# Opening stage of a two-block transformer kernel: two of eight row blocks by float32r passes, context read last, x normed before its modulation, squares folded by additions

## What is computed

```python
m_lat = (jax.nn.silu(c) @ ada_w[l] + ada_b[l])[:, None]
m_ctx = jax.nn.silu(c_ctx) @ ada_w[l] + ada_b[l]
sh1, sc1, g1, sh2, sc2, g2 = jnp.split(m_lat, 6, axis=-1)
csh1, csc1, cg1, csh2, csc2, cg2 = jnp.split(m_ctx, 6, axis=-1)
h_lat = rmsnorm(x, norm_g[l, 0]) * (1.0 + sc1) + sh1
h_ctx = rmsnorm(ctx_s, norm_g[l, 0]) * (1.0 + csc1) + csh1
z = h @ w_in
```

## Time and profile before

| | |
|---|---|
| median of three runs | 3205.82 us (3204.47 to 3207.77) |
| profiled execution | 3206.09 us, span 3204.3 us |
| PE busy | 3103.4 us, 97% of the span |
| DVE, ACT, POOL busy | 1615.0, 949.7, 1656.5 us |
| first matmul of `first_pair` | 48.07 us after the start |
| first matmul of chunk 2 | 67.78 us after the start |

### The profile page before, as it was taken

The page is one execution under the profiler, slowest core; times in us unless marked ns, Lnnn a source line. Parts: engine busy times, 40 slices in busy tenths (PEclk is TensorE's granted clock), DMA queues, the critical chain, the costliest instruction groups (busy, mean ns, idle before and its releaser), DMA issues.

```text
span 3204.3 us, 40755 instructions
## 1 busy us (share of the span) xinstructions
PE 3103.4 (97%) x15496; PEld 2574.4 (80%) x15496; DVE 1615.0 (50%) x2488; ACT 949.7 (30%) x1707; POOL 1656.5 (52%) x880
## 2 busy tenths in 40 slices
PE   8998889999999998999999999999999999999998
PEld 4887778888999766888878888788888788888887
DVE  4897768722332775211147767435531466645521
ACT  3124431111353463111122355322211314732210
POOL 2441045666787404566646633466665663066664
PEclk9999999999999999999999999999999999999999
DMA  5531026632454201233222211233332222033231
GB/s 221 191 124 44 9 84 244 241 117 88 149 180 153 66 7 66 72 98 104 99 76 92 93 46 40 66 98 93 98 110 89 89 96 68 10 97 95 94 110 67
DMA packets 84552, 319.29 MB, mean 100 GB/s; under 512 B 9200, under 2 KB 10864, under 8 KB 83376
## 3 DMA queue, kind: packets, MB, share of 16 engines
q1 hardware_dynamic: 84400, 317.20, 30.1%
HBM read 315.06 MB, written 2.10 MB: 99 GB/s over the span
## 4 chain that ended last, share of the span: by engine, by line
PE 83%; DVE 8%; issue 3%; ACT 2%; DMA 2%; POOL 1%; SPq 0%; DVEq 0%; POOLq 0%; ACTq 0%
PE two L388 15%; PE two L390 15%; PE two L389 15%; PE two L537 7%; PE two L538 7%; PE two L539 7%; DMA ada_raw<-ada 2%; PE two L2460 1%; DVE ada_junk L1120 1%; PE two L1729 1%; PE two L3060 1%; PE two L3062 1%; PE two L3061 1%; PE two L2595 1%; PE two L2620 1%
## 5 line engine op out<-in xcount | busy, mean ns | idle before, releaser
L388 PE MATMUL two<-h_hi,w_hi 128*128 128x512 f32 x2096 | 824.6, 393 | 1.8 <-DVE h_lo L2341 1.0
L390 PE MATMUL two<-h_hi,w_lo 128*128 128x512 f32 x2096 | 815.7, 389 | 0.0
L389 PE MATMUL two<-h_lo,w_hi 128*128 128x512 f32 x2000 | 778.4, 389 | 0.0
L303 POOL TENSOR_TENSOR w_lo<-w_raw,w_hi 128x1024 fp32r<-128x1024 f32 x292 | 713.5, 2445 | 41.5 <-ACT w_hi L414 11.7
L297 POOL TENSOR_SCALAR w_hi<-w_raw 128x1024 fp32r<-128x1024 f32 x272 | 291.7, 1073 | 666.4 <-issue 322.1
L388 PEld LDWEIGHTS two<-h_hi,w_hi 128*128 128x128 f32 x2096 | 393.6, 188 | 88.8 <-issue 3.9
L390 PEld LDWEIGHTS two<-h_hi,w_lo 128*128 128x128 f32 x2096 | 393.5, 188 | 81.9
L389 PEld LDWEIGHTS two<-h_lo,w_hi 128*128 128x128 f32 x2000 | 375.6, 188 | 77.9 <-issue 1.4
L505 POOL TENSOR_SCALAR w_hi<-w_raw 128x1408 fp32r<-128x1408 f32 (+1 forms) x104 | 132.5, 1274 | 426.7 <-PE two L539 308.2
L509 POOL TENSOR_TENSOR w_lo<-w_raw,w_hi 128x1408 fp32r<-128x1408 f32 (+1 forms) x110 | 327.0, 2974 | 40.0 <-DVE z L2223 16.5
L537 PE MATMUL two<-hid_hi,w_hi 128*128 128x512 f32 x704 | 274.1, 389 | 0.0
(11 more groups left out here) (633 smaller groups left out, 5713.6 us busy)
## 6 DMA issues: line engine op xcount, KB each, us to landing
w_raw<-w_f0u SPq DMA_DIRECT2D x88, 512.0 KB, 3.6
row_raw<-ada SPq DMA_DIRECT2D x48, 512.0 KB, 4.4
w_raw<-w_ssm SPq DMA_DIRECT2D x48, 512.0 KB, 3.5
w_raw<-w_f0d SPq DMA_DIRECT2D x32, 704.0 KB, 4.0
w_raw<-w_f1u SPq DMA_DIRECT2D x44, 512.0 KB, 3.5
w_raw<-w_f2u SPq DMA_DIRECT2D x44, 512.0 KB, 3.5
w_raw<-w_f3u SPq DMA_DIRECT2D x44, 512.0 KB, 3.5
ada_raw<-ada SPq DMA_DIRECT2D x32, 512.0 KB, 3.6
```

Of the source, the lines that this page charges most:

```text
L303: nc.gpsimd.tensor_tensor(lo[:, 0:self.kt], w_raw[j][:, 0:self.kt], hi[:, 0:self.kt].bitcast(f32), ALU.subtract).then_inc(split_done, 1)
L388: nc.tensor.matmul(dst, w_h[:, k], hi, start=kk == 0, stop=False)
L389: nc.tensor.matmul(dst, w_h[:, k], lo, start=False, stop=False)
L390: last = nc.tensor.matmul(dst, w_l[:, k], hi, start=False, stop=kk == self.parts * self.kt - 1)
```

## The change

It touches only the work up to the end of `first_pair`. Row blocks 4 and 6 are split: ACT rounds each quarter to float32r, DVE subtracts, and PE multiplies both parts by four columns `c_four` (the silu columns rounded, and the rest of their rounding). Every row result has four rows now, so the turn is done by f32 matmuls with a 4 x 2 matrix `row_pair` that adds rows in pairs, in place of transposes. `x` is read one block later, the first two weight chunks are read in `Start`, and the context comes behind them. DVE folds the squares of `x` by three additions and multiplies `x` by its reciprocal root in advance (`x_norm`). `FirstApply` lets ACT form `h_hi` from `x_norm` directly, and puts the context's squares between; POOL folds them, and PE sums them inside `first_pair` behind latent tile 5. ACT rounds weight chunk 0.

```diff
+                        if not (isinstance(i, int) and RAW * i + j < self.preloaded):
+                            sp.dma_start(w_raw[j][:, 0:self.kt], src).then_inc(raw_ready[j], 16)
...
+                        if isinstance(i, int) and n == SPL:
+                            self.side.pool(pool)
...
+                        if (not self.hi_act or a == 0) and not (isinstance(i, int) and n < self.rounded):
...
+                            if rhs is self.rhs:
+                                self.side.pe_first(pe, k)
...
+        SPLIT_ROWS = (4, 6)
...
             def sp(self, sp):
                 for k in range(ND):
-                    if k == 2:
+                    if k == 3:
                         sp.dma_start(x[:, :, :], xT.rearrange("(k p) t -> p k t", p=P)).then_inc(self.x_in[0], 16)
-                    if k == 4:
-                        sp.dma_start(xc[:, :, :], ctxT.rearrange("(k p) t -> p k t", p=P)).then_inc(self.xc_in[0], 16)
                     sp.dma_start(ada_n[k][:], ada0n[k:k + 1].rearrange("o p f -> (o p) f")).then_inc(self.w_in[k][0], 16)
+                for j in range(2):
+                    sp.dma_start(w_raw[j][:, 0:8], self.w[j:j + 1].rearrange("o p k f -> (o p) k f")).then_inc(raw_ready[j], 16)
+                sp.dma_start(xc[:, :, :], ctxT.rearrange("(k p) t -> p k t", p=P)).then_inc(self.xc_in[0], 16)
...
             def pe(self, pe):
-                pe.wait_ge(*upto(self.c_ready, 1))
+                pe.wait_ge(*upto(self.c_ready, 3))
                 for k in range(ND):
-                    pe.wait_ge(*upto(self.w_in[k], 16))
+                    split = k in SPLIT_ROWS
+                    if not split:
+                        pe.wait_ge(*upto(self.w_in[k], 16))
                     for q in range(4):
-                        last = nc.tensor.matmul(ps[q][0:2, :], c_silu[:, k], ada_n[k][:, 512 * q:512 * q + 512], start=k == 0, stop=k == ND - 1)
-                        if k == ND - 1:
-                            last.then_inc(self.in_ps[0], 1)
+                        cols = slice(512 * q, 512 * q + 512)
+                        if split:
+                            pe.wait_ge(*upto(self.hi, self.piece(k, q)))
+                            nc.tensor.matmul(ps[q][0:4, :], c_four[:, k], ada_hi[k][:, cols], start=False, stop=False)
+                            pe.wait_ge(*upto(self.lo, self.piece(k, q)))
+                            nc.tensor.matmul(ps[q][0:4, :], c_four[:, k], ada_lo[k][:, cols], start=False, stop=False)
+                        else:
+                            last = nc.tensor.matmul(ps[q][0:4, :], c_full[:, k], ada_n[k][:, cols], start=k == 0, stop=k == ND - 1)
+                            if k == ND - 1:
+                                last.then_inc(self.in_ps[0], 1)
                     if k == 4:
                         pe.wait_ge(*upto(self.folded, 1))
-                        nc.tensor.matmul(ps[6][:], ones[:], x_sum[:], start=True, stop=True).then_inc(self.sums[0], 1)
-                    if k == 6:
-                        pe.wait_ge(*upto(self.folded, 2))
-                        nc.tensor.matmul(ps[7][:, 0:TC], ones[:], xc_sum[:], start=True, stop=True).then_inc(self.sums[0], 1)
+                        nc.tensor.matmul(ps[6][:], ones[:], x_sq[:, 0], start=True, stop=True).then_inc(self.summed[0], 1)
                 for q in range(4):
                     pe.wait_ge(*upto(self.copied, q + 1))
                     for n in range(4 * q, 4 * q + 4):
-                        last = nc.tensor.transpose(ps[4][:, 2 * n:2 * n + 2], ada_row[:, n * P:(n + 1) * P], ident[0:2, 0:2])
+                        last = nc.tensor.matmul(ps[4][:, 2 * n:2 * n + 2], ada_row[:, n * P:(n + 1) * P], row_pair, start=n == 0, stop=True, skip_group_check=True)
...
+            def ctx_sum(self, pe):
+                pe.wait_ge(*upto(self.c_folded, 3))
+                nc.tensor.matmul(ps[7][:, 0:TC], ones[:], xc_sq[:, 0], start=True, stop=True).then_inc(self.c_summed[0], 1)
+            def pool_fold(self, pool):
+                pool.wait_ge(*upto(self.xc_squared, 4))
+                for i, n in enumerate((4, 2, 1)):
+                    nc.gpsimd.tensor_tensor(xc_sq[:, 0:n], xc_sq[:, 0:n], xc_sq[:, n:2 * n], ALU.add).then_inc(self.c_folded[0], 1)
+                    pool.wait_ge(*upto(self.c_folded, i + 1))
+            def ctx_square(self, act, i):
+                act.wait_ge(*upto(self.xc_in, 16))
+                nc.scalar.activation(xc_sq[:, 2 * i:2 * i + 2], xc[:, 2 * i:2 * i + 2], ACT.Square, scale=1.0 / 32).then_inc(self.xc_squared[0], 1)
+            def ctx_rstd(self, act):
+                act.wait_ge(*upto(self.c_summed, 1))
+                astep(nc.scalar.activation(ps[7][:, 0:TC], ps[7][:, 0:TC], ACT.Ln, bias=epsv[:, 0:1]))
+                nc.scalar.activation(ps[7][:, 0:TC], ps[7][:, 0:TC], ACT.Exp, scale=-0.5).then_inc(self.rstd_c[0], 1)
...
+                def rounded(k):
+                    act.wait_ge(*upto(self.w_in[k], 16))
+                    for q in range(4):
+                        cols = slice(512 * q, 512 * q + 512)
+                        nc.scalar.copy(ada_hi[k][:, cols], ada_n[k][:, cols]).then_inc(self.hi[0], 1)
                 act.wait_ge(*upto(self.x_in, 16))
-                nc.scalar.activation(x_sq[:, :, :], x[:, :, :], ACT.Square, scale=1.0 / 32).then_inc(self.sq[0], 1)
-                act.wait_ge(*upto(self.xc_in, 16))
-                nc.scalar.activation(xc_sq[:, :, :], xc[:, :, :], ACT.Square, scale=1.0 / 32).then_inc(self.sq[0], 1)
-                act.wait_ge(*upto(self.sums, 1))
-                astep(nc.scalar.copy(x_sum2[:], ps[6][:]))
+                for i in range(2):
+                    nc.scalar.activation(x_sq[:, 4 * i:4 * i + 4], x[:, 4 * i:4 * i + 4], ACT.Square, scale=1.0 / 32).then_inc(self.sq[0], 1)
+                rounded(4)
+                act.wait_ge(*upto(self.summed, 1))
+                nc.scalar.copy(x_sum2[:], ps[6][:])
                 astep(nc.scalar.activation(ps[6][:], ps[6][:], ACT.Ln, bias=epsv[:, 0:1]))
-                sig(nc.scalar, nc.scalar.activation(ps[6][:], ps[6][:], ACT.Exp, scale=-0.5), self.rstd)
-                act.wait_ge(*upto(self.sums, 2))
-                astep(nc.scalar.activation(ps[7][:, 0:TC], ps[7][:, 0:TC], ACT.Ln, bias=epsv[:, 0:1]))
-                sig(nc.scalar, nc.scalar.activation(ps[7][:, 0:TC], ps[7][:, 0:TC], ACT.Exp, scale=-0.5), self.rstd_c)
+                nc.scalar.activation(ps[6][:], ps[6][:], ACT.Exp, scale=-0.5).then_inc(self.rstd[0], 1)
+                rounded(6)
                 for q in range(4):
+                    if q == 1:
+                        act.wait_ge(raw_ready[0], 16)
+                        nc.scalar.copy(w_hi[0][:, 0:8], w_raw[0][:, 0:8]).then_inc(hi_done, 1)
                     act.wait_ge(*upto(self.in_ps, q + 1))
-                    nc.scalar.copy(ada_row[:, 512 * q:512 * q + 512], ps[q][0:2, :]).then_inc(self.copied[0], 1)
+                    nc.scalar.copy(ada_row[:, 512 * q:512 * q + 512], ps[q][0:4, :]).then_inc(self.copied[0], 1)
...
+                def rest(k):
+                    for q in range(4):
+                        cols = slice(512 * q, 512 * q + 512)
+                        dve.wait_ge(*upto(self.hi, self.piece(k, q)))
+                        nc.vector.tensor_tensor(ada_lo[k][:, cols], ada_n[k][:, cols], ada_hi[k][:, cols].bitcast(f32), ALU.subtract).then_inc(self.lo[0], 1)
                 dve.wait_ge(*upto(self.sq, 2))
-                nc.vector.tensor_reduce(xc_sum[:], xc_sq[:, :, :].rearrange("p k t -> p t k"), AX.X, ALU.add).then_inc(self.folded[0], 1)
+                vstep(nc.vector.tensor_tensor(x_sq[:, 0:4], x_sq[:, 0:4], x_sq[:, 4:8], ALU.add))
+                vstep(nc.vector.tensor_tensor(x_sq[:, 0:2], x_sq[:, 0:2], x_sq[:, 2:4], ALU.add))
+                nc.vector.tensor_tensor(x_sq[:, 0], x_sq[:, 0], x_sq[:, 1], ALU.add).then_inc(self.folded[0], 1)
+                rest(4)
+                dve.wait_ge(*upto(self.rstd, 1))
+                for k in range(ND):
+                    if k == 2:
+                        rest(6)
+                    last = nc.vector.tensor_tensor(x_norm[:, k], x[:, k], ps[6][:], ALU.mult)
+                vstep(last)
...
+                act.wait_ge(*upto(self.start.mods, 1))
+                for k in range(ND):
+                    nc.scalar.activation(h_hi[:, k], x_norm[:, k], ACT.Identity, scale=self.gain(k), bias=self.shift(k)).then_inc(self.hi_ready[0], 1)
+                    if 1 <= k < 5:
+                        self.start.ctx_square(act, k - 1)
+                self.start.ctx_rstd(act)
+            def dve(self, dve):
+                for k in range(ND):
+                    v = ps[2 + k % 2][:]
+                    nc.vector.tensor_scalar(v, x_norm[:, k], self.gain(k), self.shift(k), ALU.mult, ALU.add).then_inc(self.scaled[0], 1)
+                    dve.wait_ge(*upto(self.scaled, k + 1))
+                    dve.wait_ge(*upto(self.hi_ready, k + 1))
```

(67 more changed lines are left out.)

12 lines of the change are left out of this document (6 added, 6 removed).

## The result

| | before | changed |
|---|---|---|
| median, 20 executions each | 3206.05 us (3203.71 to 3210.98) | 3211.03 us (3207.57 to 3215.03) |
| mean of all executions in this study | 3207.40 ± 0.19 (126) | 3210.94 ± 0.39 (34) |
| profiled execution | 3206.09 us | 3209.37 us |
| chunk 2 starts | 67.78 us | 68.69 us |

(The ± is one standard error.) The ratio is 1.0013 [1.0007, 1.0019]: slower by 0.13%. That lies within 0.2%, to which the prediction gave a chance of 0.93, but 3211.03 is 2.2 us above the top of the range and 4.3 above the predicted time. The profiled execution of before belongs to its early half: the single times of that kernel spread from 3203 to 3211 and are thinnest between 3206 and 3207 (9 of 126). The median of 20 falls beside that gap and moves easily, so the means, 3.5 ± 0.4 us apart, are the better measure.

What follows compares the result with a forecast made beforehand. PE, busy 97% of the span, was taken as the bound, any shift of chunk 2 carried one for one. S 0.9 us late on 3206.09 gave 3207.0, or 3206.7 for the median; range 3203.6 to 3208.8.

Steps and rivals of the forecast that it cites:

- Transfers, PE up to E: Opening: x lands at 20.1 us, block 4 takes 26.1 to 31.1 waiting for DVE, E at 42.05 against 43.72.
- E: The end of row block 7 on PE: 43.72 us before the change, forecast 42.05.
- E to T: Sixteen turning matmuls in place of transposes: bounds 1.11 and 3.57 us, the upper one taken.
- T: DVE's first work with mods: 45.59 us before the change, forecast 46.4, 0.8 late.
- T to PE's start: Scaling beside h_hi (0.72 us), then a 0.69 subtraction: T + 1.5, PE's first large matmul at 47.9 against 48.07.
- The disputed hold by POOL: DVE's x_norm scaling at 46.4 us beside POOL's last subtraction: 0 or 0.6 us on PE's start, by two readings.
- The context: In first_pair: POOL's fold takes 4.5 us to 57.1, then PE's sum and ACT's root; S 0.5 to 1.2 late.
- S: DVE's first context scaling: 58.28 us before, forecast 58.8 to 59.5, 0.9 late taken; chunk 2 follows by 9.5.
- the wait for POOL's fold that I had named as a sign: In first_pair behind latent tile 5: PE waits up to 1 us for POOL's fold before the context's sum.
- The second rival: Opening: POOL holds the scaling (0.6 us), PE's gap in block 4 brings slow pace (up to 1.2); 3208.4, chance 0.17.
- a different spacing behind chunk 2: Sign of being wrong: behind chunk 2's start the forecast assumed that nothing changes.
- the first rival: Turns cost as transposes, S up to 1.5 us early; 200 to 400 us perhaps another 1 to 2; 3203.9, chance 0.28.

Runs made afterwards that it cites:

- numbers 6: The changed kernel with only row block 4 split, block 6 done as the other f32 blocks; mean 3211.0 ± 0.6 us, ratio to before 1.0012.
- 7: The changed kernel with only row block 6 split, block 4 done as the other f32 blocks; mean 3206.8 ± 0.7 us, ratio to before 1.0001.
- number 9: The changed kernel with only block 6 split and PE waiting ahead of block 4 for the last fold of x; mean 3211.3 ± 0.9 us, ratio 1.0013.

## Why the prediction was wrong

**Transfers, PE up to E: right, and a little pessimistic.** x landed at 19.36 and not 20.1, block 3 kept nobody waiting (its matmuls ended at 25.4, not 26.1), and block 6 took 2.45 us. So E was 40.60, where I had 42.05. That block 4 is bound by DVE and takes longer, not shorter, was right: 25.4 to 30.2, 4.8 us (forecast 5.0). The balance behind the forecast adds up to 1.3 and not to the 1.65 that it names; E itself was added up step by step and does not rest on it.

**E to T: right.** The turns took 3.67 us (forecast 3.57; 0.23 us a product): the upper bound, from the rows of the same operation, was the right choice. T came at 45.10, 1.3 us ahead of the forecast and 0.49 ahead of the kernel before (forecast 0.8 behind it), for E's sake alone.

**T to PE's start: two durations small.** The scaling of x_norm into PSUM took 0.81 and `h_hi` 0.80, against my 0.52 to 0.77 and 0.72, so T + 1.76 and not T + 1.5. The disputed hold by POOL did not occur: L1549 took 0.81 at 45.10, beside POOL's subtraction that ran to 45.44, and 0.81 at 46.75 with POOL idle. VectorE: DVE Perf Modes, section Mode 2x_2P, in the Trainium skill, keeps the two-port mode to operands in SBUF; the trace agrees, as this scaling into PSUM took the same 0.81 us beside POOL and without it.

**The context: right in sum, partly by luck.** The fold took 4.59 us (forecast 4.5) and was over before PE asked. What held S was PE: after its gap of 2.60 us it had 1.2 GHz for the first ten passes, and reached the context's sum at 57.20, inside my 56.1 to 57.8. S came at 58.83, 0.55 behind the kernel before and not 0.9, and chunk 2 followed it by 9.86 us and not 9.50. That chunk 2 was 0.91 late, as forecast to a hundredth of a microsecond, is luck: PE's start was 1.0 us ahead of the forecast, the slow pace took 2.0 us (ten passes at 0.43 in place of 0.23), and the wait for POOL's fold that I had named as a sign did not come.

**The second rival's price: too rarely counted, not wrong.** The clock fell inside block 4 in two of five profiles, for 1.0 to 1.4 us in the opening (forecast up to 1.2). I had treated it as an alternative with 0.17; it is a cost that every series of executions carries a share of. The average opening is 1.7 us late and not 0.9: about 0.5 of that is this clock fall, the rest is that the single 67.78 stood 0.3 above the kernel's average.

**The step that failed** is the first: "From there on PE, ACT, DVE and POOL depend on each other and on transfers that landed long before, so I carry any shift of that point to the end one for one." The prediction named a different spacing behind chunk 2 as a sign of being wrong, and that is what came. The order of instructions is fixed, but PE's clock is not: from 264 to 381 us the same instructions have a short course near 116 us and a long one near 121. The kernel before took the short one in its four profiles and, as its times in two groups suggest, the long one in others; the changed kernel took the long one in five profiles of five. I had named this stage in the first rival, as a gain only. The two courses probably also explain the base: 3205.82, the median of three, and the profile of 3206.09 were early executions of a kernel whose mean is 3207.4, so a forecast set against them started 1.5 us low.

**What stays open** is what selects the course. It is not the delay alone: chunk 2 at 71.67 and 68.91 went with the short course, 68.45 and 64.50 with the long one. That splitting block 4 costs (numbers 6 and 7) and that delaying it does (number 9) is shown in the means; whether it matters through the opening, through the choice of the course or both is only partly so: of the 4.2 us between numbers 6 and 7, the profiles show 2.7 in the opening.

## What to carry to other kernels

A split that halves the work of an engine helps only if its inputs are made in time: here PE saved 1.6 us of passes in block 4 and waited 2.2 us for the first of them, and dropping that split alone (number 7) was worth 4.1 ± 0.8 us in the mean. Look for the wait that an idle engine could have prevented: ACT stood 3 to 6 us ahead of the row copies, and drawing one rounding and the context's squares and sum forward brought chunk 2 1.7 us closer. And before a shift of a microsecond is carried through 3 ms, take several profiles of the unchanged kernel: one execution and a median of three hid a spread of 8 us.
